# Retention heads 1 to 7 form values and gates side by side, with seven products for eight in three of eight k-tile pairs; VectorE makes all sums of raw weights

## The reference, cut to what matters

```
proj = x @ w_in                       # 2048 x 12288
q, k, v, gate = split(proj)           # 8 heads: 256, 256, 512, 512 columns each
o = retention(rotary(q), rotary(k), v)
y = group_norm_heads(o) * silu(gate)
out = layer_norm(ALPHA * x + y @ w_out)
```

## Time and profile before

| | us |
|---|---|
| median of 3 runs (2363.45 to 2364.28) | 2363.5 |
| profiled execution | 2361.91 |
| its span | 2360.1 |
| TensorE busy | 2344.1 |
| VectorE busy | 1618.9 |
| ScalarE busy | 1215.5 |
| GpSimd busy | 424.1 |

### The profile page before, as it was taken

The page is one execution under the profiler, slowest core; times in us unless marked ns, Lnnn a source line. Parts: engine busy times, 40 slices in busy tenths (PEclk is TensorE's granted clock), DMA queues, the critical chain, the costliest instruction groups (busy, mean ns, idle before and its releaser), DMA issues.

```text
span 2360.1 us, 30013 instructions
## 1 busy us (share of the span) xinstructions
PE 2344.1 (99%) x11846; PEld 1975.4 (84%) x11846; DVE 1618.9 (69%) x2008; ACT 1215.5 (52%) x1631; POOL 424.1 (18%) x368
## 2 busy tenths in 40 slices
PE   9999999999999999999999999999999999999999
PEld 7878898888888888888788888887888888888887
DVE  7997578779877777875765656658666655666656
ACT  6876454445544444475655555535444443444542
POOL 1271016326423223400000000001000000000000
PEclk9999999999999999999999999999999999999999
DMA  8655655655665556565566565565655666556653
GB/s 298 196 193 192 214 174 194 191 187 182 212 201 189 188 188 211 199 202 175 179 191 210 163 210 164 178 187 166 197 181 181 217 188 198 180 181 188 185 179 125
DMA packets 127614, 450.38 MB, mean 191 GB/s; under 512 B 14289, under 2 KB 18017, under 8 KB 126961
## 3 DMA queue, kind: packets, MB, share of 16 engines
q1 hardware_dynamic: 127472, 448.46, 59.2%
HBM read 446.26 MB, written 2.15 MB: 190 GB/s over the span
## 4 chain that ended last, share of the span: by engine, by line
PE 95%; DVE 3%; ACT 1%; issue 0%; DMA 0%; POOL 0%; SPq 0%; DVEq 0%; ACTq 0%
PE bank L875 94%; DVE wlo L1747 1%; PE bank L1024 0%; DVE ev L1750 0%; DVE hn L1750 0%; PE bank L1205 0%; PE bank L1276 0%; DVE X L1760 0%; DVE hT L1747 0%; PE bank L1224 0%; DMA hT<-in_xT 0%; DVE S L1747 0%; ACT whi L1290 0%; DVE xa L1747 0%; DVE xa L1750 0%
## 5 line engine op out<-in xcount | busy, mean ns | idle before, releaser
L1747 DVE TENSOR_TENSOR wlo<-raw,whi 128x1024 fp32r<-128x1024 f32 (+2 forms) x811 | 1043.5, 1294 | 644.2 <-ACT whi L1290 642.6
L1290 ACT ACTIVATE whi<-raw 128x1024 fp32r<-128x1024 f32 (+2 forms) x813 | 846.5, 1047 | 878.5 <-PE bank L875 843.2
L875 PE MATMUL bank<-xa,whi 128*128 128x512 f32 (+1 forms) x2688 | 841.6, 395 | 8.5 <-DVE xa L1750 3.4
L875 PE MATMUL bank<-whi,xa 128*128 128x512 f32 x2048 | 639.1, 393 | 2.2 <-DVE wlo L1747 1.8
L875 PEld LDWEIGHTS bank<-xa,wlo 128*128 128x128 f32 x2656 | 497.7, 188 | 115.1
L875 PE MATMUL bank<-xa,wlo 128*128 128x256 f32 (+1 forms) x2656 | 521.1, 278 | 0.0
L875 PEld LDWEIGHTS bank<-whi,xa 128*128 128x128 f32 x2048 | 379.8, 188 | 80.0 <-DVE wlo L1747 2.4
L875 PE MATMUL bank<-whi,xb 128*128 128x512 f32 x1416 | 437.1, 390 | 0.0
L875 PEld LDWEIGHTS bank<-xa,whi 128*128 128x128 f32 x2688 | 410.5, 188 | 16.8 <-issue 10.2
L875 PE MATMUL bank<-wlo,xa 128*128 128x512 f32 x1024 | 399.4, 390 | 0.0
L875 PEld LDWEIGHTS bank<-whi,xb 128*128 128x128 f32 x1416 | 264.8, 188 | 55.3 <-DVE wlo L1747 0.3
(11 more groups left out here) (277 smaller groups left out, 1576.5 us busy)
## 6 DMA issues: line engine op xcount, KB each, us to landing
raw<-in_w SPq DMA_DIRECT2D x803, 512.0 KB, 3.8
hn<-row_sums SPq DMA_DIRECT2D x16, 256.0 KB, 3.8
hT<-in_ln_rows SPq DMA_DIRECT2D x2, 2048.0 KB, 8.1
raw<-in_w SPq DMA_DIRECT2D x9, 256.0 KB, 3.2
S<-in_x SPq DMA_DIRECT2D x4, 512.0 KB, 8.4
hT<-in_x SPq DMA_DIRECT2D x1, 2048.0 KB, 8.0
S<-row_sums SPq DMA_DIRECT2D x16, 128.0 KB, 4.5
out<-S SPq DMA_DIRECT2D x8, 256.0 KB, 2.5
```

Of the source, the lines that this page charges most:

```text
L875: return pe.matmul(o, w, x, start=start, stop=stop, skip_group_check=True)
L1290: act.activation(hi, r, ACT.Copy).then_inc(*w_high(i))
L1747: return dve.tensor_tensor(o, x, y, op)
```

## The change

Three things. First, for heads 1 to 7 the values and gates of a head come from one matrix `ret_vg` whose 1024 columns are 512 of values and 512 of gates. `paired_head(h)` lays them out: five plain pieces of values, two plain pieces of gates, three groups (k-tile pairs 0, 1, 2) of upper, lower, pair_sums and full_sums one behind the other, then three plain pieces of gates. Behind them stand `rq` and `rk`, then the next head. The sums of the tokens for the three pairs are made once, by GpSimd, in head 0. The values are folded by one copy on ScalarE and six operations on VectorE at the piece behind the last group, and split at the next; the gates get one addition each and a silu in place. `ret_gate` and `ret_turn` move to e+7 and e+8.

Second, the step `sums` moves from GpSimd to VectorE, also in down0 and down1; it is attached at a-4 (down0, heads) and a-5 (down1) in place of a-7.

Third, to make room: the last layer's rows are held in `hn` instead of `sn`, and the last gain and bias rows are loaded behind head 7 instead of head 2.

```diff
+HEAD_PAIRS = (0, 1, 2)
+PAIRED_HEADS = (1, 2, 3, 4, 5, 6, 7)
+GATE_LEAD, GATE_TAIL = 2, 3
...
-                late(max(a - 7, begun + 2) if k else a - 7, "sums", a)
+                late(max(a - 5, begun + 2) if k else a - 4, "sums", a)
...
+    def paired_head(h):
+        v, g = (begin(kind, h, xa4, "natural", 512) for kind in ("rv", "rgate"))
+        rest = [p for p in range(8) if p not in HEAD_PAIRS]
+        spread = rest[GATE_LEAD:len(rest) - GATE_TAIL]
...
+        for p in rest:
+            use(v, "ret_vg", 1024 * h, 2 * p, 2, p == rest[0], False)
+        for p in rest[:GATE_LEAD]:
+            use(g, "ret_vg", 1024 * h + 512, 2 * p, 2, p == rest[0], False)
+        for i, p in enumerate(HEAD_PAIRS):
+            first, last = i == 0, i == len(HEAD_PAIRS) - 1
+            a = part("upper", 2 * p, first)
+            late(a - 4, "sums", a)
+            part("lower", 2 * p + 1, first)
+            part("pair_sums", 2 * p, first)
+            d = part("full_sums", 2 * p, first, last)
+            if i < len(spread):
+                use(g, "ret_vg", 1024 * h + 512, 2 * spread[i], 2, False, False)
+        late(d + 1, "fold", "rv", h, d)
+        late(d + 2, "rv_split", h)
+        for p in rest[len(rest) - GATE_TAIL:]:
+            u = use(g, "ret_vg", 1024 * h + 512, 2 * p, 2, False, p == rest[-1])
+        return u
...
+            if h == 0:
+                for i, p in enumerate(HEAD_PAIRS):
+                    mix(e + 2 + 3 * i, 2, p)
+            if h in PAIRED_HEADS:
+                late(e + 7, "ret_gate", h)
+                late(e + 8, "ret_turn", h)
+            else:
+                e = block("rgate", h, xa4, "ret_w_in", 4 * D + 512 * h, nat, "natural", 512)
+                late(e + 1, "ret_gate", h)
+                late(e + 2, "ret_turn", h)
+            if h == 7:
+                late(e + 1, "load_rows", 1)
...
                     if uses[before].part == "upper":
-                        q.wait_ge(*pool_val.of("sum", before, 2))
+                        q.wait_ge(*vec_val.of("sum", before, 2))
                     elif uses[before].part == "lower":
-                        q.wait_ge(*pool_val.of("sum", before - 1, 4))
+                        q.wait_ge(*vec_val.of("sum", before - 1, 4))
...
+                    elif step == "sums":
+                        a, = k
+                        pair, full = sums[uses[a].block.kind, uses[a].block.arg]
...
+                        tt(pair[:, 0:512], above[:, 0:512], above[:, 512:1024], ALU.add).then_inc(*vec_val("sum", a, 1))
+                        q.wait_ge(*landed(a + 1))
+                        tt(pair[:, 512:1024], above[:, 512:1024], below[:, 512:1024], ALU.add).then_inc(*vec_val("sum", a, 2))
+                        q.wait_ge(*vec_val.of("sum", a, 1))
+                        tt(full[:, 0:512], pair[:, 0:512], below[:, 512:1024], ALU.add).then_inc(*vec_val("sum", a, 3))
+                        q.wait_ge(*vec_val.now())
+                        tt(full[:, 512:1024], full[:, 0:512], below[:, 0:512], ALU.add).then_inc(*vec_val("sum", a, 4))
...
+                    elif step == "fold" and k[0] == "rv":
+                        _, h, d = k
+                        n = tile_of["rv", h]
+                        q.wait_ge(*act_evac.of("first", "rv", h))
+                        tt(rg[:, 0, :], bank[7][:, :], rv_sum[0], ALU.subtract).then_inc(*vec_val("less", "rv", h))
+                        q.wait_ge(*vec_val.now())
+                        tt(rv_sum[1], rg[:, 0, :], bank[4][:, :], ALU.add).then_inc(*vec_val("fold", "rv", h, 0))
+                        q.wait_ge(*piece_tile.of("tile", n))
+                        tt(rv_sum[0], rv_sum[0], bank[n % 4][:, :], ALU.add).then_inc(*vec_evac("tile", n))
+                        q.wait_ge(*vec_val.of("fold", "rv", h, 0))
+                        tt(rg[:, 1, :], rv_sum[1], bank[6][:, :], ALU.add).then_inc(*vec_val("fold", "rv", h, 1))
+                        q.wait_ge(*vec_val.now())
+                        q.wait_ge(*piece_tile.of("tile", n + 1))
+                        tt(rv_sum[1], bank[(n + 1) % 4][:, :], rv_sum[1], ALU.subtract).then_inc(*vec_evac("tile", n + 1))
+                        tt(rg[:, 0, :], rg[:, 0, :], bank[6][:, :], ALU.add).then_inc(*vec_val("folded", "rv", h))
```

More of the change, by code:

```diff
@@ L495, in pieces_in_order @@
         mats[f"pool{g}"] = x["pool_w"][0, g]
+    values, gates = (mats["ret_w_in"][:, c * D:c * D + 2 * D].reshape(D, 8, 512) for c in (2, 4))
+    mats["ret_vg"] = np.concatenate([values, gates], axis=2).reshape(D, 8 * 1024)
     flat, xT = [], x["x"][0].T
@@ L697, in block_kernel @@
         start_of = {s.block: u for u, s in reversed(list(enumerate(uses)))}
[L698 removed]
+        by_act = {b.tile + j for b in {s.block for s in uses} for j in range(b.tiles)
+                  if b.kind in ("ple", "pgate", "fv") or b.kind == "rgate" and b.arg not in PAIRED_HEADS}
         LAST_SUMS = max([i for i, s in enumerate(uses) if s.part in SUMS and s.block.kind == "down0"], default=-1)
@@ L1498, in scalar_program @@
                         q.wait_ge(*pool_val.of("mixed", half, p, 4))
-                        if half and p not in EARLY[1]:
+                        if half == 2:
+                            q.wait_ge(*piece_tile.of("used", ends["fox_out"]))
+                        elif half and p not in EARLY[1]:
                             q.wait_ge(*piece_tile.of("used", XA_FREE[1]))
@@ L2178, in vector_program @@
                             tt(x[:, T:2 * T], vbuf[f % 4], f32(x[:, 0:T]), ALU.subtract).then_inc(*x_low("ff", f))
+                    elif step == "sums":
+                        a, = k
+                        pair, full = sums[uses[a].block.kind, uses[a].block.arg]
+                        earlier = [i for i, s in enumerate(uses[:a]) if s.part == "full_sums"]
+                        if earlier:
+                            q.wait_ge(*w_low.of(earlier[-1]))
+                        if uses[a].first and uses[a].block.kind != "rv":
+                            q.wait_ge(*(x_low.of("ff", 21 if uses[a].block.arg else 0) if uses[a].block.kind == "down0"
+                                        else piece_tile.of("used", XA_FREE[1])))
+                        above, below = [raw[turn_of[i] % NRAW] for i in (a, a + 1)]
+                        q.wait_ge(*landed(a))
+                        tt(pair[:, 0:512], above[:, 0:512], above[:, 512:1024], ALU.add).then_inc(*vec_val("sum", a, 1))
[5 more added lines that the diff above has]
+                        tt(full[:, 512:1024], full[:, 0:512], below[:, 0:512], ALU.add).then_inc(*vec_val("sum", a, 4))
                     elif step == "mixed_low":
@@ L2559, in pool_program @@
                         tt(v[3], lower[:, 0:128], v[1], ALU.subtract).then_inc(*pool_val("mixed", half, p, 4))
[L2560 to L2564, removed]
-                            q.wait_ge(*w_low.of(earlier[-1]))
-                        if uses[a].first:
-                            q.wait_ge(*(x_low.of("ff", 21 if uses[a].block.arg else 0) if uses[a].block.kind == "down0"
-                                        else piece_tile.of("used", XA_FREE[1])))
-                        up, low = [raw[turn_of[i] % NRAW] for i in (a, a + 1)]
-                        q.wait_ge(*landed(a))
-                        tt(pair[:, 0:512], up[:, 0:512], up[:, 512:1024], ALU.add).then_inc(*pool_val("sum", a, 1))
-                        q.wait_ge(*landed(a + 1))
-                        tt(pair[:, 512:1024], up[:, 512:1024], low[:, 512:1024], ALU.add).then_inc(*pool_val("sum", a, 2))
-                        q.wait_ge(*pool_val.of("sum", a, 1))
-                        tt(full[:, 0:512], pair[:, 0:512], low[:, 512:1024], ALU.add).then_inc(*pool_val("sum", a, 3))
-                        q.wait_ge(*pool_val.now())
-                        tt(full[:, 512:1024], full[:, 0:512], low[:, 0:512], ALU.add).then_inc(*pool_val("sum", a, 4))
                     elif step == "fold_end" and k[0] == "down1":
```

101 lines of the change are left out of this document (73 added, 28 removed).

## The result

The changed kernel takes **2391.7 us** (median of 4 runs, 2388.2 to 2392.5), the kernel before 2363.5 beside it. The ratio is 1.0115, 95% interval 1.0103 to 1.0128: slower by 28 us. I had forecast slower, 2375.6 us, in a range from 2357 to 2386; the sign was right, the size was not. The profiled execution took 2392.5 us (span 2390.7), 30.6 more than the profiled one of before.

The account below looks back on a forecast made before the run. TensorE was taken to bound the kernel, busy 2344.1 of 2360.1 us. A saving of 14.3 us against waits of 6.2 (turn), 9.0 (third pair sums) and 11.2 (fold) gave +12.1, 2375.6 us, range 2357 to 2386.

Parts of the forecast that it names:

- The saving: Heads 1 to 7: three groups each save one product of 0.68 us on TensorE's path, 14.28 us in all.
- Sums on VectorE, 2.52 a group: Heads: VectorE's four sums of raw weights take 2.52 us a group, bounds 2.40 and 2.88.
- Down0 and down1 at nothing: Down stages: moving GpSimd's twelve groups of sums to VectorE neither wins nor loses time.
- (a) the turn: Heads 2, 3, 5, 6, 7: TensorE waits 1.17 us ahead of the transposes, 5.9 us, plus 0.3 behind heads 3 and 7.
- half as wide: At the turn: the short upper's narrower split lets VectorE start the gated values about 0.14 us before the second gate piece ends.
- (b) the third pair sums: Third group: TensorE waits for VectorE's split, 1.4 us in heads 1 and 4, 1.24 in five others, 9.0 us.
- (c) the fold: First rq piece, seven heads: TensorE waits 1.6 us for the second bank, emptied behind a memory-bound split, 11.2 us.
- 3.6 us pass: Third rq piece: time from a raw buffer's release to ScalarE's start, 3.6 us, with landing possibly 3.2 or 4.2.
- I expect no change of clock: TensorE's granted clock stays, no wait exceeding the earlier longest of 3.0 us; effect 0.
- Mixtures of head 0 at nothing: Head 0: GpSimd's three token mixtures run under the gate block, 20 us ahead of use, and cost nothing.
- The rivals: Lead holds, 2349.2 us (0.13); fold's wait vanishes, 2364.4 (0.18); VectorE bounds down too, 2400 or 2388 (0.07).
- Half of the waits: First rq piece: the fold's wait vanishes, the other waits remain, +0.9 us, 2364.4 us; chance 0.18.

Follow-up runs that it names:

- The version with all moves: Changed kernel with the fold ahead of the split, gate block one piece earlier, a plain gate piece between groups, head 0's mixtures two pieces later: 2353.5 us.
- the first experiment: Kernel before with only the sums of raw weights in down0 and down1 moved from GpSimd to VectorE: 2363.9 us.
- a piece between the groups: Changed kernel with the fold ahead of the split and one full gate piece moved from the tail to between the first and second group: 2370.1 us.
- the thin sums: Changed kernel with the four sums of raw weights in the heads cut from 512 to 8 columns: 2367.1 us.
- the filler: Changed kernel with six unused matmuls into an idle bank ahead of the first rq piece of heads 1 to 7: 2386.7 us.
- the last two experiments: Kernel with all four moves, head 0's GpSimd mixtures four pieces earlier (2356.6 us), or made to wait for TensorE's scores (2352.7 us).
- two groups a head: Kernel with all four moves, but two seven-for-eight groups in a head instead of three: 2356.8 us.
- the early mixtures: Kernel with all four moves, but head 0's GpSimd mixtures placed four pieces earlier: 2356.6 us.

## Why the prediction was right or wrong

- *The saving*, 14.3 us: right, as far as runs show it. The version with all moves is 10.0 under the kernel before (medians), and 1.2 is lost in head 0. The fold costs more than its idle time of 1.2: in the seven heads the first matmul into the second bank and the one behind it start 0.34 to 0.82 and 0.34 us after the one ahead, against 0.235 without a wait, together 2.9 us too late. 14.3 - 2.9 - 1.2 is 10.2.
- *Sums on VectorE, 2.52 a group*: the rows of the changed kernel have 1.29 and 1.41 for two and two, 2.53 from the first to the split (1708.25 to 1710.78). *Down0 and down1 at nothing*: right, TensorE 54.40 busy of 54.40 and 410.00 of 410.00, and the first experiment. In the fold an addition that waits for its predecessor starts 0.72 after it (1795.33 to 1796.05), an independent one 0.60. The Trainium skill, VectorE: DVE Perf Modes (The DRAIN you can't avoid), measured on a row of copies that the semaphores between them cost nothing; for these additions the trace does not agree.
- *(a) the turn*: right in place, heads and size (1.12 idle, 1.17 forecast). The experiment with a piece between the groups bore out the "half as wide" on which it hung.
- *(b) the third pair sums*: right (1.37 and 1.11 against 1.4 and 1.24), and the thin sums and the spread piece show its cause.
- *(c) the fold*: the mechanism was right, the size was not: 17.8 instead of 11.2. The term that was mis-sized is the landing, "3.6 us pass": 3.95 to 4.85, 4.56 in the mean, which over seven heads is 6.7 us more and all of the difference. I took it from one load that was issued alone (median of such loads 3.54); the loads here come in a bunch, which my own count of the splits (three of 1.14 in a row) already said.
- *"I expect no change of clock"*: the step that failed, 7.8 us. I argued from the longest wait of the kernel before, 3.0 us, and from a clock of 1.00 in the head, a stretch that has no waits. Behind that wait the clock indeed stayed at 1.00. But the trace of before has a second long wait, and behind its 2.76 us the clock is 0.58.

```profile
143.47 1.30 PE L875 MATMUL bank<-xa,whi 128*128 128x512 f32 x2 [2.76 <-DVE X L1760]
```

```profile
144.00:147.00 3.00, 3.00 (x12) 2.62 (x12) 3.00 (x3) 0.00 (x0) 2.84 (x3) 0.58 0.77 226
```

  The fold's two waits, 2.2 us together in head 1, are nearer to that than to none. The 1.6 of my forecast lies between 1.38 (head 2, no fall) and 1.80 (head 7 with the filler, a fall): the late loads made the waits long enough, and the clock then added its part.
- *Mixtures of head 0 at nothing*: wrong by 1.2 us. Their cover was to be the gate block, but GpSimd waits for nothing and runs the first at once, at 1663, beside VectorE's rotation: two additions take 2.10 us instead of 0.75. I used just this effect to explain the 8.01 us of the earlier trace rows and did not look where the new GpSimd work would fall. The Trainium skill, SBUF — State Buffer (Who interferes with whom), has the rule of the two engines' shared port, and the last two experiments agree with it: the pair takes 2.11 us beside GpSimd's mixtures and 0.75 without them, wherever they are put.
- *The range*: the 2392 that I gave as the end of the forecast alone is near the measured 2391.7 by luck. It came from every wait at its bound, 2.9 us for (b) above all, which measured 1.37 and 1.11; the clock was not in it.
- *The rivals*: none held. "Half of the waits" had the fold's wait vanish; moved by one place in the queue, it did, and gave 2367.1 against the 2364.4 written there.

## What to carry to other kernels

When a shorter algorithm makes TensorE wait, look where the late operation stands in its engine's queue before giving the idea up: here the order of the fold, the gate block and one plain piece turned 1.2% slower into 0.4% faster with the same work. Price a wait of about 2 us as more than itself, here 1.6 us more in most cases: look in the trace of before at the granted clock behind waits of that length. And take a load's landing time from a stretch where loads are issued as densely as the change will issue them.

## What the runs showed of the hardware

- In the heads TensorE's clock fell to its lower level behind waits of 2.1 us, and also behind two waits with one matmul between (1.11 and 0.76 in head 5 the shortest of the changed kernel; 0.98 and 0.82 with the filler). It did not behind 1.4 or less (head 2: 0.62 and 0.76). Above that it is not certain: 1.22 and 0.76 in head 3, one of the five waits of 2.07 and 2.08, waits of 2.10 to 2.14 at 176 us in three profiles, and the one of 2.33 with the early mixtures were followed by 1.00. Each fall cost 1.55 to 1.6 us. What decides between equal waits stays open.
- The wait of 2.76 to 2.81 us at 144 us stands in all twelve profiles; a low clock follows it in nine, and none in three (the filler, the piece between the groups, two groups a head).
- In the first 20 us the wait of about 3 us was followed by a clock of 0.56 in the changed kernel's profile and by 1.00 in that of before. Head 0's scores, ahead of which the kernels of nine profiles do the same work, start between 1664.85 and 1666.33 us: executions differ by some 1.5 us before the heads. The three earliest are those three without a low clock up to there.
- A load of 512 KB took longer from issue to landing the more of its kind were under way: 3.55, 3.74, 4.50 and 5.46 us (medians) with none, one, two and three.
- Two VectorE additions of 128x256 take 0.75 us, and 2.10 beside GpSimd's.
